# Value-like projections with the activations stationary, from 256 to 512 moving weight columns

## The reference

```python
z = h @ w_in[l]                                   # first block
q_a, k_a, v_a, q_b, f_b, i_b, og_b, gate_a, gate_b = jnp.split(z, split_at, axis=-1)
v_a = v_a.reshape(att_shape)                      # 1536 columns: dilated attention
o_b = hgrn2_recurrence(q_b..., f_b..., i_b..., lb_all[l])   # i_b: 1024 columns
...
proj = h @ w_in[layer]                            # second block
(qa, ka, va, qb, kb, vb, qi, ki, wi, qc, kc, vc) = jnp.split(proj, split_points, axis=-1)
oa = moba_attention(qa, ka, va); ob = dsa_attention(qb, kb, vb, qi, ki, wi)
oc = stick_breaking_attention(qc, kc, vc)         # va, vb, vc: 1024 columns together
```

## Time and profile before

| what | value |
| --- | --- |
| time, median of 3 runs | 2987.23 us (2981.62 to 2991.45) |
| span of the profiled execution, first to last instruction | 2978.1 us |
| median of the runs less that span | 9.1 us |
| PE busy | 2913.8 us, 98% of the span |
| DVE busy | 2112.5 us, 71% |
| ACT busy | 1314.2 us, 44% |
| mean granted clock of TensorE | 0.987 |

### The profile page before, as it was taken

The page is one execution under the profiler, slowest core; times in us unless marked ns, Lnnn a source line. Parts: engine busy times, 40 slices in busy tenths (PEclk is TensorE's granted clock), DMA queues, the critical chain, the costliest instruction groups (busy, mean ns, idle before and its releaser), DMA issues.

```text
span 2978.1 us, 52377 instructions
## 1 busy us (share of the span) xinstructions
PE 2913.8 (98%) x23186; PEld 2848.8 (96%) x23196; DVE 2112.5 (71%) x2680; ACT 1314.2 (44%) x1300; POOL 213.1 (7%) x163
## 2 busy tenths in 40 slices
PE   9999999999999999999999999999999999999999
PEld 8999999999999999999999999998889999987999
DVE  7777876556777777876656777777866777778644
ACT  5334545454334344545444334335643343446432
POOL 0000430000000000420000000003000000030000
PEclk9999999999999999999999999999999999999999
DMA  7664433445665654333435664663246656531453
GB/s 269 238 225 157 154 126 131 156 149 192 241 240 212 248 205 170 142 137 121 165 145 207 247 234 186 240 225 128 85 172 253 227 218 249 184 142 72 156 183 143
DMA packets 78465, 549.07 MB, mean 184 GB/s; under 512 B 8480, under 2 KB 11936, under 8 KB 12320
## 3 DMA queue, kind: packets, MB, share of 16 engines
q1 hardware_dynamic: 67152, 464.99, 43.6%
q0 software_dynamic: 11088, 80.75, 6.8%
HBM read 544.65 MB, written 1.05 MB: 183 GB/s over the span
## 4 chain that ended last, share of the span: by engine, by line
PE 80%; DVE 13%; ACT 3%; issue 2%; POOL 2%; DMA 0%; DVEq 0%; POOLq 0%; SPq 0%; ACTq 0%
PE ps L301 73%; DVE ring_lo L295 4%; ACT w_hi L288 2%; PE ps L373 1%; PE ps L510 1%; PE ps L789 1%; POOL qk L1540 1%; DVE hk L1244 1%; POOL rope_a L1536 1%; DVE e L378 1%; PE ps L919 0%; PE ps L1636 0%; DVE e L1302 0%; DVE e L1301 0%; DVE a_hg L1322 0%
## 5 line engine op out<-in xcount | busy, mean ns | idle before, releaser
L295 DVE TENSOR_TENSOR ring_lo<-ring,w_hi 128x2048 fp32r<-128x2048 f32 x438 | 1008.6, 2305 | 588.9 <-ACT w_hi L288 585.5
L301 PE MATMUL ps<-h_hi,w_hi 128*128 128x256 f32 x4560 | 1310.5, 287 | 14.3 <-DVE h_lo L410 8.9
L301 PE MATMUL ps<-h_lo,w_hi 128*128 128x256 f32 x4560 | 1296.7, 284 | 0.0
L301 PE MATMUL ps<-h_hi,ring_lo 128*128 128x256 f32 x4560 | 1296.1, 284 | 0.0
L288 ACT ACTIVATE w_hi<-ring 128x2048 fp32r<-128x2048 f32 x438 | 836.9, 1911 | 779.2 <-PE ps L301 696.1
L301 PEld LDWEIGHTS ps<-h_hi,w_hi 128*128 128x128 f32 x4560 | 881.9, 193 | 23.3 <-issue 14.8
L301 PEld LDWEIGHTS ps<-h_lo,w_hi 128*128 128x128 f32 x4560 | 882.2, 193 | 3.2 <-issue 2.4
L301 PEld LDWEIGHTS ps<-h_hi,ring_lo 128*128 128x128 f32 x4560 | 881.7, 193 | 0.0
L301 PE MATMUL ps<-g_hi,w_hi 128*128 128x256 f32 x1408 | 398.5, 283 | 0.0
L301 PE MATMUL ps<-g_lo,w_hi 128*128 128x256 f32 x1408 | 398.5, 283 | 0.0
L301 PE MATMUL ps<-g_hi,ring_lo 128*128 128x256 f32 x1408 | 398.5, 283 | 0.0
(11 more groups left out here) (319 smaller groups left out, 3329.2 us busy)
## 6 DMA issues: line engine op xcount, KB each, us to landing
ring<-stream SPq DMA_DIRECT2D x438, 1024.0 KB, 4.8
e<-ada POOLq DMA_DIRECT2D x77, 1024.0 KB, 5.1
x<-x_t SPq DMA_DIRECT2D x4, 256.0 KB, 4.3
mem<-mem_t SPq DMA_DIRECT2D x1, 1024.0 KB, 9.4
out_t<-x SPq DMA_DIRECT2D x4, 256.0 KB, 2.1
con_sb<-con SPq DMA_DIRECT2D x1, 896.0 KB, 14.8
con_sb<-con SPq DMA_DIRECT2D x1, 640.0 KB, 6.1
hq<-lmask SPq DMA_DIRECT2D x1, 512.0 KB, 15.5
```

The source lines that it names most:

```text
L295: nc.vector.tensor_tensor(ring_lo[:, p % RING, :], ring[:, p % RING, :], w_hi[:, p % HIGHS, :].bitcast(F32), ALU.subtract).then_inc(S.w_lo ...
L301: mm = nc.tensor.matmul(out, a, b, start=start and n == 0, stop=stop and n == 2, skip_group_check=group)
```

## The change

The value-like tiles are cut in another way. A tile used to hold 256 output columns over the whole contraction of 1024; now it holds 512 output columns over half of the contraction (four of the eight steps k), and two tiles make a pair with 512 result columns for both groups of 128 tokens. The matmuls of such a tile move 512 columns, so a tile has 24 of them in place of 48. A pair fills two PSUM banks, and neither is finished before the second tile's last matmuls: in the first tile (half 0) each token group writes its bank, in the second (half 1) it adds to it. So ACT evacuates nothing behind the first tile of a pair and two banks (a token group's 512 columns each) behind the second. The waits for free banks move into half 0, one per bank. In ACT's program of `M_I` the table load and the logarithm now follow the first pair, not the first tile. The host lays the weights out accordingly. Stream length, DMA sizes, `high`, `low` and the number of evacuations stay.

```diff
+        def project_half(pe, p, half, banks, src, free=None):
+
+            pe.wait_ge(S.w_lo_ready, p + 1)
+            for t in range(2):
+                if half == 0:
+                    pe.wait_ge(S.evac_done, nth(S.evac_done, free + t))
+                for k in range(4):
+                    mm = triple(ps[:, banks[t], :], both(src, 4 * half + k, t * P, (t + 1) * P),
+                                weights(p, k * 512, (k + 1) * 512), half == 0 and k == 0, half == 1 and k == 3)
+            mm.then_inc(S.tile_done, 1)
...
-            for n in range(1, 12):
+            for n in range(1, 8):
                 if n >= 3:
                     pe.wait_ge(S.evac_done, nth(S.evac_done, n - 2))
-                (project_tok if n >= 8 else project)(pe, MIX + n, n % 3, h2)
+                project(pe, MIX + n, n % 3, h2)
+            for n in (8, 10):
+                for half in range(2):
+                    project_half(pe, MIX + n + half, half, (n % 3, (n + 1) % 3), h2, n - 2)
...
-                    pe.wait_ge(S.evac_done, nth(S.evac_done, 12 + n - 2))
-                    (project if n < 12 else project_tok)(pe, M_QK + n, (12 + n) % 3, h2)
+                    if n < 12:
+                        pe.wait_ge(S.evac_done, nth(S.evac_done, 12 + n - 2))
+                        project(pe, M_QK + n, (12 + n) % 3, h2)
+                    else:
+                        a = 12 + 2 * i
+                        project_half(pe, M_QK + n, n % 2, (a % 3, (a + 1) % 3), h2, a - 2)
...
-            evac(M_I, hi[:, :, 0:T], 8 % 3)
+            def evac_pair(p, out, bank):
+
+                for half in range(2):
+                    act.wait_ge(S.tile_done, p + half + 1)
+                    if half == 1:
+                        for t in range(2):
+                            nc.scalar.activation(out[:, t, :], ps[:, (bank + t) % 3, :],
+                                                 ACT.Copy).then_inc(S.evac_done, 1)
+                    high(act, p + half + HIGHS)
+
+            evac_pair(M_I, hi[:, :, 0:512], 8 % 3)
             nc.scalar.preload_act_table_set("natural_log_exp_and_others")
             act.wait_ge(S.forget_ready, nth(S.forget_ready, 1))
             nc.scalar.activation(hb[:], hb[:], ACT.Ln).then_inc(S.log_ready, 1)
-            for n in range(1, 4):
-                evac(M_I + n, hi[:, :, n * T:(n + 1) * T], (8 + n) % 3)
+            evac_pair(M_I + 2, hi[:, :, 512:1024], 10 % 3)
...
+                if 7 <= n < 11:
+                    a = 7 if n < 9 else 9
+                    project_half(pe, p, n - a, (a % 3, (a + 1) % 3), h2, a - 2)
+                    return
...
-                elif 7 <= n < 11:
-                    project_tok(pe, p, n % 3, h2)
...
-                    nc.scalar.activation(val[:, :, (n - 7) * T:(n - 6) * T], src, ACT.Copy).then_inc(S.evac_done, 1)
+                    if n in (8, 10):
+                        for t in range(2):
+                            nc.scalar.activation(val[:, t, (n - 8) * T:(n - 6) * T], ps[:, (n - 1 + t) % 3, :],
+                                                 ACT.Copy).then_inc(S.evac_done, 1)
```

More of the change, by code:

```diff
@@ L1039, in one_act @@
                     decay(i)
+                if 2 * i >= 12:
+                    evac_pair(M_QK + 2 * i, val[:, :, (2 * i - 12) * T:(2 * i - 10) * T], (12 + 2 * i) % 3)
+                    continue
                 for n in (2 * i, 2 * i + 1):
[L1041 to L1044, removed]
+                    turn(n)
+                    evac(M_QK + n, qk[:, 2 * n:2 * n + 2, :], (12 + n) % 3)
             def gate(n):
@@ L2301, in by_columns, with by_halves @@
     return w.reshape(KD, P, n, T).transpose(2, 1, 0, 3).reshape(n, P, TILE)
+def by_halves(w):
+    n = w.shape[1] // 512
+    return w.reshape(2, 4, P, n, 512).transpose(3, 0, 2, 1, 4).reshape(2 * n, P, TILE)
 def by_ffn(gate, up, down):
@@ L2321, in layer_one @@
     for part in (fb, qb, ib, q, k, v, og, ga, gb, a["w_hgrn_branch"][l]):
-        tiles += list(by_columns(part))
+        tiles += list(by_halves(part) if part is ib or part is v else by_columns(part))
     tiles += list(a["w_att_branch"][l].reshape(HEADS, P, 2, 512).transpose(2, 1, 0, 3).reshape(2, P, TILE))
@@ L2344, in layer_two @@
     tiles = by_ffn(a["ffn_w1_2"][l, 0], a["ffn_w3_2"][l, 0], a["ffn_w2_2"][l, 0])
-    for w_ in (part["qi"], ki, part["qb"], part["kb"], part["qa"], part["ka"], part["va"], part["vb"],
-               part["vc"]):
+    for w_ in (part["qi"], ki, part["qb"], part["kb"], part["qa"], part["ka"]):
         tiles += list(by_columns(w_))
+    tiles += list(by_halves(np.concatenate([part["va"], part["vb"], part["vc"]], axis=1)))
     for q, k in zip(by_columns(part["qc"]), by_columns(part["kc"])):
```

## The result

The changed kernel takes 2997.62 us (median of 16 runs, 2995.28 to 3000.28) against 2986.95 for the one before (16 runs, 2981.31 to 2993.75): ratio **1.0037**, 95% interval 1.0029 to 1.0045, slower by 10.7 us. The profiled execution has a span of 2995.4 us and a mean granted clock of 0.982; that of before had 2978.1 and 0.987. The execution profiled for before was one of its fast ones (2978.1 us of span, where the runs' median is 2986.95 and a run's time is some 2 us above its span).

The account below looks back on a forecast made before the run. PE is the chain from the V tiles on, but DVE is later at M_I and tiles 7 and 8. Per layer +4.3 (M_I, clock), -3.2 (M_V), -1.16 (Z_V); two layers -0.1 us: 2987 us, no change, range 2978 to 2998.

Parts of the forecast that it names:

- the sum for `M_V`: First block, V tiles, PE the chain: three pairs gain 0.9, 1.16 and 1.16 us, -3.2 us a layer.
- the room of 2.1 us before level 6: V rounds: level 6's factors end at 401.5, the level starts at 403.61, so an earlier PE still finds them ready.
- the case that the stretch of the earlier trace falls away: V rounds: without the fall at M_QK, the half clock in the first V pair goes too: 2980 us.
- rival (d): More half-clock stretches than today, as PE idles longer before tile 9 or in the rounds: 2990 to 2997 us, chance 0.10.
- What a matmul costs: Wide tiles: 216 ns per 512-column matmul against 120 ns per narrow one, so each tile gains 0.58 us.
- The argument from the float32 matmul: Float32 matmul of 256 columns, array busy as for 512, takes 216 ns with its load hidden; taken for the wide matmul.
- The one from the half clock: Narrow matmuls at half clock take 214 ns, so columns need at most 107 ns; speaks against 13 ns added to each.
- M_I: First block: PE's 2.3 us gain worthless; logarithm behind two evacuations makes DVE's scan wait 2.1 us, M_QK starts late.
- the line "between the ends": Alternative at 227 ns: tile gains 0.31, logarithm costs 2.65, V gives 1.7, Z 0.6; +2.5 a layer pair, 2992 us.
- The clock at M_QK: After 5.7 us of PE idling, M_QK runs about 5.0 us at half clock, costing 2.2 us a layer.
- Z_V: Second block: tiles 7 and 8 gain nothing, DVE being later; tiles 9 and 10 gain 1.16 us a layer.
- Rival (a): Wide matmuls: width worth nothing, moving operand arriving at 120 ns per 256 columns; 2998 us, +0.36%, chance 0.10.

Follow-up runs that it names:

- e3: Kernel before with only the M_V tiles in the new wide form: 2985.47 us, ratio 0.9993.
- e9: Kernel before with Z_V wide, each 512 columns split into 384 and 128 (sum incomplete, for intervals only): 2996.16 us, one run.
- e2: Kernel before with only the M_I tiles in the new wide form: 2999.27 us, ratio 1.0027.
- e4: Kernel before with only the Z_V tiles in the new wide form: 2984.65 us, ratio 0.9987.
- e1: Changed kernel, all tiles wide, with table load and logarithm moved back behind the first tile of M_I: 2988.32 us, ratio 0.9997.
- e6: Kernel before with Z_V in matmuls of 128 columns, 96 a tile: 3029.32 us, one run.
- e7: Kernel before with M_V and Z_V wide, M_I as before: 2983.44 us, ratio 0.9988.
- e5: Changed kernel with 22 unused bf16 matmuls of zeros filling PE's wait before M_QK: 2989.00 us, ratio 1.0007.
- e8: e7 plus zero matmuls in PE's waits, 4 before M_QK, 3 and 5 before levels 4 and 5: 2980.54 us, ratio 0.9981.

## Why the prediction was wrong

The forecast was no change, 2987 us; the kernel is 0.37% slower, at the upper edge of the range. The step that failed most is the sum for `M_V`, -3.2 us a layer: measured are +1.9 and +0.3 us (from level 5 to level 8 it is 50.51 us for 48.60 in the first layer, 48.93 for 48.66 in the second). Of the 9.2 us by which the parts miss the forecast of -0.1 us, 8.6 lie there.

- *M_V*: two things went wrong. The size: 0.62 us a pair instead of 1.16. At 227 ns the prediction itself has 1.7 a layer, and e3 shows 1.6. And the clock, which was taken as it lay in the one trace of before: the room of 2.1 us before level 6 was there because level 5 and the first pair ran at half clock for 6.8 us. With the clock up PE is at level 6 too early even with narrow tiles (1.07 us in e9), and what the wide pair gains there only lengthens the wait (1.64 us). Behind it came half clock, for 2.9 us more in level 6 and 2.2 in the pair in the first layer, 2.6 and 0.9 in the second. The prediction names a fall of the clock at `M_QK` and the case that the stretch of the earlier trace rows falls away, to 2980 us, but its sum has no new one at level 6. More such stretches are rival (d), which had 0.10 and 2990 to 2997 us. It isn't the lateness of 4.3 us that uses up the room, since level 5 and the factors of level 6 are late by the same.
- *What a matmul costs*: the wide matmul was mis-sized, 216 ns taken and **227** measured. The 13 ns above the columns are added at 256, 384 and 512 columns; 128 are bound by the load. The argument from the float32 matmul was wrong in that it took the 13 ns for a load that comes out from behind short columns. The one from the half clock held for the half clock alone: 427 ns there, with nothing added, and 13 ns at the full one. A tile gains 0.31 us and not 0.58. The Trainium skill, TensorE: Matmul & The Clock Gate, section "Back-to-back issue gap", has N/2.4 + 2.5 ns for a matmul by itself and about 131 ns for 512 columns in a stream with loads; at full clock the runs agree with neither, and its 81 ns for 128 columns in such a stream stands against the 111 measured here. As the section keeps the load out of its N/2.4 + 2.5 ns, the prediction's sentence that by it the load is hidden reads too much into it.
- *M_I*: the mechanism was right in each link (worthless gain on PE, logarithm behind two evacuations, scan, remainder, `M_QK`). The wait measured 2.52 us for 2.1; the line "between the ends" had 2.65 for 227 ns.
- *The clock at M_QK*: it fell, for 3.4 us of `M_QK` in the first layer instead of 5.0, and cost 1.5 us instead of 2.2 (1.6 in the second layer). In the trace of e2 it was the 2.3 us of the forecast, behind the same pause of 5.08 us.
- *Z_V*: tiles 7 and 8 gain nothing, right; the pauses behind them grew by 0.26 and 0.27 us, which takes 0.53 of the 0.62 us that they give at 227 ns. Tiles 9 and 10: 0.6 us instead of 1.16. e4's -1.1 at equal clock is the 4 x 0.31 of two layers.
- *The sum*: by the two traces 5.9 + 4.4 in the first block and -0.6 a layer in the second, 9.1 us, beside the 10.7 measured. The rest is not assigned; the two executions also differ in how much half clock they have elsewhere. Rival (a) named the right time, 2998, by luck: the width is worth half of what was forecast, not nothing.

What stays open: why the half clock falls in and behind level 5 in some passes and behind level 6 in others. In the six traced passes of after, e1 and e2, in which the clock fell at `M_QK`, it was level 6 each time; in the twelve of before, e3, e4, e6, e7 and e9, in which it had not, seven times level 5 and five times level 6. That the fall at `M_QK` brings about the one at level 6 would fit, and is not shown. Open, too, is where the 13 ns come from. They are there between fp32r matmuls at full clock and not at half clock, and 2 to 3 ns in the float32 ones; contention between the load and the moving columns would fit, and was not tried. And open is why e1 stands 2.4 us above e7 at equal clock, when its trace shows nothing lost but PE's pause and the half clock.

## What to carry to other kernels

Before counting a gain against the room in front of a wait, ask what made the room. Here it was half clock, which lay there in one execution and elsewhere in the next; with the clock up there was no room but a wait, and the gain was lost in it. A delay that shifts both sides of a wait leaves the room as it is. A trace is one execution: traces of variants that leave a stretch of code alone are further executions of it, and here they showed the second way that the only trace of before hid. Count a pause on PE twice: for itself, and for the half clock that may follow, here 1.5 us behind one of 5.1 us and 3.5 to 5 us of level and tile behind one of 1.6. A wider matmul saved 13 ns of each pair of narrow ones and nothing else, which paid only where PE was the chain (e7), and was lost where it moved a step that another engine waits for.

## What the runs showed of the hardware

- fp32r matmuls with a new stationary operand each: 111, 120, 173 and 227 ns for 128, 256, 384 and 512 columns at full clock, 214 and 427 for 256 and 512 at half clock.
- The granted clock was 0.50 behind pauses of PE of 5.08 and 2.47 us (before `M_QK`, in both layers of after and e1) and behind pauses of 1.07 (e9) and 1.64 us (after) before level 6; it was 1.00 behind the 1.23 us of before, behind 1.65 us in e5's first layer and 1.64 in e8's second. So which pauses are followed by it isn't a matter of their length alone. Zero matmuls in bf16 in a pause of 5 us kept it at 1.00 (e5).
- The spread of 14 us between executions of the kernel before goes with this clock: 2.6 us for each 0.001 of its mean, with 1.1 us left.
